# Transformer layer on one core: one pair of k tiles of the up-projection as seven products instead of eight, with weight sums built by DMA

## The chip, the cores and the metric

The kernel runs on one core of a Trainium2 chip. The metric is the device time of one execution in microseconds, the median of three runs; lower is better.

## What is computed

One layer over 256 tokens of width 2048: RMSNorm and one input projection, sixteen attention heads in two kinds, an output projection with residual, and a gated MLP with a causal depthwise convolution of width 3 between up-projection and activation. The change lies in the MLP's first product, `h @ w_up`:

```
def conv_ffn(x, norm2_g, w_up, conv_w, conv_b, w_down):
    h = rms_norm(x, norm2_g)
    u = h @ w_up                      # (256 x 2048) @ (2048 x 11008)
    u = conv over the tokens, width 3, per column, + conv_b
    gate, val = jnp.split(u, 2, axis=-1)
    return x + (jax.nn.silu(gate) * val) @ w_down
```

## The kernel before

All weights stream through one ring. A piece is 128 rows (one k tile) of up to 1024 float32 columns, 512 KB. SyncE (SP) loads it into one of four slots of `raw`; ScalarE copies it, rounded, to `w_hi` (`split_hi`); VectorE writes the rest to `w_lo` (`split_lo`); TensorE multiplies high by high, high by low and low by high, three matmuls for each product of a 128x128 block of tokens with 512 columns. Four counters order this. SP loads piece g once piece g-4 is split (`split_done`). ScalarE copies piece g once TensorE has used piece g-4 (`piece_used`). VectorE follows ScalarE, and TensorE waits for `split_done`. Each engine runs its instructions in the order in which they are written.

The pieces come in this order: 128 of the input projection, eight for each of the sixteen heads (2 x 384 columns each); 32 of the output projection; then the up-projection in eleven batches. A batch is four tiles of the gate columns and four of the value columns, 512 + 512 columns in a piece, and runs over 16 k tiles; the eleventh has 384 + 384. For each piece TensorE does 2 token blocks (m) x 2 column halves (gate, value) x 3 = 12 matmuls of 512 columns, into four PSUM banks. The banks alternate between two sets of four (`UP_BANKS`), by the batch's parity. Batches 3 to 8 run in a hardware loop, the others are written out.

While TensorE works on batch nb, ScalarE and VectorE also finish batch nb-1, by a list of steps in which step s also splits piece s+4: ScalarE takes the four banks to `ut` scaled by the norm `r2` (`evacuate_up`, steps 0 and 1), VectorE transposes 32x32 blocks (`turn_up`, steps 1 and 2), ScalarE moves them to their place (`move_up`, 16 instructions, steps 2 to 9), then both do the convolution (`conv_tap2`, `conv_taps`), silu and gate times value. The down-projection follows, which already takes nine pairs of its pieces as seven products, with sums built on VectorE.

GpSimd (POOL) is used for a few small operations in the first heads and has issued no DMA.

## Time and profile before

| | |
|---|---|
| median of 3 runs | 1038.23 us (1037.99 to 1040.0) |
| the profiled execution, its own time | 1039.86 us |
| its span in the profile | 1038.1 us |
| TensorE busy | 99% of the span |
| VectorE, ScalarE busy | 77%, 77% |
| GpSimd busy | 2% |
| granted TensorE clock | 1.0 throughout |
| moved by DMA | 221.04 MB, mean 213 GB/s |

A matmul's record is longer than the step from one to the next, since they are pipelined; the step is read from the starts. The same holds a little for ScalarE and VectorE. Times inside the span count from its start.

### The profile page before, as it was taken

The page shows a single profiled execution, that of the slowest core. Times are in us where ns is not written, and L with a number is a line of the kernel's source. Part 1 is how long each engine was busy: PE and PEld are TensorE (multiplying, and loading weights), DVE is VectorE, ACT ScalarE, POOL GpSimd, SP SyncE. Part 2 cuts the span into 40 slices and gives each one's busy share as a digit, 9 for nine tenths or more (in the row PEclk, how much of TensorE's full clock was granted, in tenths as well). Part 3 has the DMA queues.
Part 4 walks back from the last instruction along what each step waited for, and adds up shares of the span by engine and source line. Part 5 has one row for each costly group of instructions (what it writes and reads, how often), then busy time and mean ns, then how long its engine had stood idle before and what let it go on. Part 6 is the DMA issues. An engine that isn't in the chain of part 4 may idle for free.

```text
span 1038.1 us, 16517 instructions
## 1 busy us (share of the span) xinstructions
PE 1031.2 (99%) x5278; PEld 931.9 (90%) x5278; DVE 801.3 (77%) x1354; ACT 799.7 (77%) x1406; POOL 21.1 (2%) x27
## 2 busy tenths in 40 slices
PE   9999999999999999999999999999999999999998
PEld 8999999999988888888888888888889988888887
DVE  7788888878766655577776776777768799989988
ACT  7776676888858885879788788797887789856753
POOL 0101010000000000000000000000000000000000
PEclk9999999999999999999999999999999999999999
DMA  9666777777766666666565565665656757656664
GB/s 351 240 199 212 216 239 229 222 252 227 249 229 201 205 194 201 204 213 201 189 218 195 193 221 190 213 203 188 216 187 190 232 182 233 201 200 218 203 203 162
DMA packets 81437, 221.04 MB, mean 213 GB/s; under 512 B 20312, under 2 KB 24544, under 8 KB 81248
## 3 DMA queue, kind: packets, MB, share of 16 engines
q1 hardware_dynamic: 81232, 220.07, 65.0%
q8 instruction: 34, 0.56, 0.2%
q10 hardware_dynamic: 144, 0.20, 0.1%
q14 instruction: 27, 0.22, 0.1%
HBM read 214.32 MB, written 5.91 MB: 212 GB/s over the span
## 4 chain that ended last, share of the span: by engine, by line
PE 87%; DVE 8%; DMA 2%; ACT 1%; issue 1%; SPq 0%; DVEq 0%; ACTq 0%
PE ps L714 14%; PE ps L713 14%; PE ps L712 14%; PE ps L501 7%; PE ps L503 7%; PE ps L502 7%; PE ps L741 4%; PE ps L743 4%; PE ps L742 4%; DVE w_lo L1314 3%; PE ps L691 3%; PE ps L693 3%; PE ps L692 3%; DMA raw<-in_wrest 2%; PE ps L523 1%; DVE sums_lo_t L1883 1%
## 5 line engine op out<-in xcount | busy, mean ns | idle before, releaser
L1314 DVE TENSOR_TENSOR w_lo<-raw,w_hi 128x1024 fp32r<-128x1024 f32 (+2 forms) x406 | 457.1, 1131 | 186.3 <-ACT w_hi L838 184.4
L838 ACT ACTIVATE w_hi<-raw 128x1024 fp32r<-128x1024 f32 (+2 forms) x406 | 393.4, 977 | 145.3 <-PE ps L714 53.1
L712 PE MATMUL ps<-w_hi,xs 128*128 128x512 f32 (+1 forms) x704 | 263.4, 374 | 0.0
L713 PE MATMUL ps<-w_lo,xs 128*128 128x512 f32 (+1 forms) x704 | 263.4, 374 | 0.0
L714 PE MATMUL ps<-w_hi,xs 128*128 128x512 f32 (+1 forms) x704 | 263.4, 374 | 0.0
L501 PE MATMUL ps<-w_hi,xs 128*128 128x384 f32 (+1 forms) x496 | 164.9, 332 | 0.1
L502 PE MATMUL ps<-w_lo,xs 128*128 128x384 f32 (+1 forms) x496 | 161.8, 326 | 0.0
L503 PE MATMUL ps<-w_hi,xs 128*128 128x384 f32 (+1 forms) x496 | 161.8, 326 | 0.0
L712 PEld LDWEIGHTS ps<-w_hi,xs 128*128 128x128 f32 x704 | 133.1, 189 | 17.2
L713 PEld LDWEIGHTS ps<-w_lo,xs 128*128 128x128 f32 x704 | 133.1, 189 | 17.2
L714 PEld LDWEIGHTS ps<-w_hi,xs 128*128 128x128 f32 x704 | 133.1, 189 | 17.2
L1174 ACT ACTIVATE uT<-utT 32x512 f32<-32x512 f32 (+1 forms) x176 | 109.4, 622 | 26.8 <-DVE utT L1742 22.8
L741 PE MATMUL ps<-w_hi,a_s 128*128 128x512 f32 (+1 forms) x274 | 103.7, 378 | 0.0
L742 PE MATMUL ps<-w_lo,a_s 128*128 128x512 f32 (+1 forms) x274 | 103.4, 377 | 0.0
L743 PE MATMUL ps<-w_hi,a_s 128*128 128x512 f32 (+1 forms) x274 | 103.4, 377 | 0.0
L501 PEld LDWEIGHTS ps<-w_hi,xs 128*128 128x128 f32 x496 | 93.7, 189 | 2.6 <-issue 1.3
L502 PEld LDWEIGHTS ps<-w_lo,xs 128*128 128x128 f32 x496 | 93.8, 189 | 0.2
L503 PEld LDWEIGHTS ps<-w_hi,xs 128*128 128x128 f32 x496 | 93.7, 189 | 0.0
L741 PEld LDWEIGHTS ps<-w_hi,a_s 128*128 128x128 f32 x274 | 51.8, 189 | 8.0 <-issue 0.8
L743 PEld LDWEIGHTS ps<-w_hi,a_s 128*128 128x128 f32 x274 | 51.8, 189 | 7.3
L742 PEld LDWEIGHTS ps<-w_lo,a_s 128*128 128x128 f32 x274 | 51.8, 189 | 7.1
L691 PE MATMUL ps<-w_hi,mixed 128*128 128x512 f32 x128 | 49.0, 383 | 0.0
(231 smaller groups left out, 1139.1 us busy)
## 6 DMA issues: line engine op xcount, KB each, us to landing
raw<-in_wrest SPq DMA_DIRECT2D x278, 512.0 KB, 4.0
raw<-in_win SPq DMA_DIRECT2D x117, 384.0 KB, 3.6
raw<-in_wrest SPq DMA_DIRECT2D x16, 384.0 KB, 3.1
p_scratch<-pdT SPq DMA_DIRECT2D x14, 192.0 KB, 2.9
p_read<-p_scratch SPq DMA_DIRECT2D x56, 48.0 KB, 2.8
xtok<-in_xtok SPq DMA_DIRECT2D x4, 512.0 KB, 13.2
xv<-in_xtok SPq DMA_DIRECT2D x4, 512.0 KB, 5.6
raw_ahead<-in_w SPq DMA_DIRECT2D x5, 392.0 KB, 8.1
```

Source lines behind the costliest of these rows:

```text
L501: pe.matmul(o, xh, wh, start=(kt == 0), stop=False, skip_group_check=True)
L502: pe.matmul(o, xh, wl, start=False, stop=False, skip_group_check=True)
L503: last = pe.matmul(o, xl, wh, start=False, stop=(kt == KT - 1), skip_group_check=True)
L712: pe.matmul(o, xh, wh, start=(k == 0), stop=False, skip_group_check=True)
L713: pe.matmul(o, xh, wl, start=False, stop=False, skip_group_check=True)
L714: last = pe.matmul(o, xl, wh, start=False, stop=(k == KT - 1), skip_group_check=True)
L741: pe.matmul(to, ah, wh, start=start, stop=False, skip_group_check=True)
L742: pe.matmul(to, ah, wl, start=False, stop=False, skip_group_check=True)
L743: return pe.matmul(to, al, wh, start=False, stop=stop, skip_group_check=True)
L838: act.activation(slot(w_hi, s, w), slot(raw, s, w), ACT.Copy).then_inc(hi_ready, 1)
L1174: act.activation(dst, src, ACT.Copy).then_inc(u_moved, 1)
L1314: dve.tensor_tensor(slot(w_lo, s, w), slot(raw, s, w), f32(slot(w_hi, s, w)), ALU.subtract).then_inc(split_done, 1)
```

## The change

In batches 1 to 8 of the up-projection, k tiles 8 and 9 are no longer multiplied as eight blocks (2 token blocks x 2 k tiles x 2 column halves) but as seven products of sums of blocks, as in Strassen's scheme. In place of two pieces of 1024 columns there are four: `left` (the left half of tile 8, 512 columns), `lower` (tile 9), and `two` and `more`, 2 x 1024 columns of sums of the weight blocks. The sums of the token blocks are the same for all batches; they are made once, in batch 0 (`h_sums`), in `kept_hi` and `kept_lo`. The weight sums are built in a DRAM scratch tensor `t_scratch` by DMAs that GpSimd issues: per batch six, each waiting for the one before (three copies and three that add to what is there). They begin when 96 pieces are used, that is with head 12, and build q (for batch q+1) also waits for 96 + 12 q used pieces. SP waits for build q (`t_built`) before it loads piece `two` of batch q+1.

Three of the seven products go into the batch's own banks; the four that belong to more than one block go to the other set of four banks. Those are read out and combined while TensorE goes on with tiles 10 to 15: ScalarE copies the first (`take_first`), VectorE does four additions (`up_sums`), ScalarE scales the result (`scale_sums`). At the batch's end VectorE takes the four own banks out with the scale and adds these (`evacuate_sums`, a `scalar_tensor_tensor`), where ScalarE did it before. The lists of steps for ScalarE and VectorE in these batches are new (`UP_ACT`, `UP_DVE`), with 18 steps instead of 16. TensorE waits for the combined sums (`c_summed`) before the next batch, and for the evacuation of the batch before (`u_evac`) ahead of tile 8. Semaphores of two norms are shared (`norm_*`) to make room, with no other effect.

```
+UP_SEVEN, UP_BATCHES = (8,), (1, 8)
+UP_ACT = dict(late_silu=5, moves=(3, 3, 4, 4, 6, 8, 10, 10), first=9, scale=(14, 16), taps=(11, 12, 15, 16), silu=(13, 17, 17))
+UP_DVE = dict(late_taps=(3, 6), late_gate=(4, 8), evacuate=(0, 0), turn=(1, 1), sums=(9, 10),
+              taps=((11, 12), (14, 14), (16, 16)), gate=(15, 16))
+BUILD_AT = 8 * (H + 4)
...
 # SP
+            def up_pieces(nb, par):
...
+                    if kind in ("two", "more"):
...
+                        if kind == "two":
+                            sp.wait_ge(t_built, 96 * (q + 1))
+                        sp.dma_start(slot(raw, s), t_d[q * P:(q + 1) * P, c:c + PW]).then_inc(raw_landed[s], 16)
 # TensorE
+            def up_seven(nb, par, k, j):
...
+                if first:
+                    pe.wait_ge(u_evac, nb * 4)
...
+                pe.wait_ge(split_done, up_first(nb) + (j + 1))
+                product(shared[0], a(0, 0), b(0, 0), first, last).then_inc(piece_used, 1)
+                pe.wait_ge(split_done, up_first(nb) + (j + 2))
+                product(own[0], a(1, 0), b(1, 0))
+                product(own[1], a_sum(3), b(1, 1)).then_inc(piece_used, 1)
+                pe.wait_ge(split_done, up_first(nb) + (j + 3))
+                product(shared[2], a_sum(1), b(2, 0), first, last)
+                product(shared[3], a_sum(0), b(2, 1), first, last).then_inc(piece_used, 1)
+                pe.wait_ge(split_done, up_first(nb) + (j + 4))
+                end = product(shared[1], a_sum(2), b(3, 0), first, last)
+                if last:
+                    end.then_inc(c_ended, 1)
+                product(own[2], a(1, 1), b(3, 1)).then_inc(piece_used, 1)
 # ScalarE
+            def take_first(nb, par):
+                act.wait_ge(c_ended, nb)
...
+                act.activation(c_tile(0, 0), bank(UP_BANKS[1 - par][0]), ACT.Copy).then_inc(c_first, 1)
+            def scale_sums(nb, m):
+                act.wait_ge(c_summed, nb * 4)
+                act.activation((x1sq, x1f)[m][:], (x1sq, x1f)[m][:], ACT.Copy, scale=r2[:, m:m + 1]).then_inc(c_scaled, 1)
 # VectorE
+            def evacuate_sums(pb, m, par):
+                dve.wait_ge(piece_used, up_first(pb) + UP_LONG)
+                dve.wait_ge(c_scaled, pb * 2 + (m - 1))
+                dve.wait_ge(u_turned, pb * 2)
+                for gv in range(2):
+                    at = (2 * m + gv) * UW
+                    dve.scalar_tensor_tensor(out=ut[:, at:at + UW], in0=bank(UP_BANKS[par][2 * m + gv]), scalar=r2[:, m:m + 1],
+                                             in1=c_tile(m, gv), op0=ALU.mult, op1=ALU.add).then_inc(u_evac, 1)
 # GpSimd
+            def build_sums(q):
...
+                pool.dma_start(block_(0, 2), upper).then_inc(t_built, 16)
+                pool.wait_ge(t_built, 96 * q + 16)
+                pool.dma_start(block_(0, 2).rearrange("p (k c) -> p k c", k=2), both[:, :, BLOCK:PW], accum_op=ALU.add,
+                               max_dma_last_dim=4096).then_inc(t_built, 16)
...
+            for q in range(UP_SUMS):
+                pool.wait_ge(piece_used, BUILD_AT + q * 12)
+                build_sums(q)
```

How the order of instructions moves, first on VectorE at the start of a batch (the static part before the loop). `w_lo` rows are `split_lo`, `utT` the transposes. Before, batch 2:

```order
L1314 TENSOR_TENSOR w_lo<-raw,w_hi 128x1024 [waits hi_ready]
L1749 SCALAR_TENSOR_TENSOR y_t<-uT,conv,y_t 128x256 [waits g_y2]
L1754 SCALAR_TENSOR_TENSOR y_t<-uT,conv,y_t 128x256 [waits g_silu,g_y1]
L1314 TENSOR_TENSOR w_lo<-raw,w_hi 128x1024 [waits hi_ready]
L1742 STREAM_TRANSPOSE utT<-ut 128x1024 [waits u_moved,u_evac]
L1314 TENSOR_TENSOR w_lo<-raw,w_hi 128x1024 [waits hi_ready]
L1742 STREAM_TRANSPOSE utT<-ut 128x1024 [waits u_moved,u_evac]
```

After the change, from the end of batch 1 (the first `w_lo` of the two) into batch 2:

```order
L1492 TENSOR_TENSOR w_lo<-raw,w_hi 128x1024 [waits hi_ready] x2
L2024 SCALAR_TENSOR_TENSOR ut<-ps,r,x1sq 128x512 [waits u_turned,c_scaled,piece_used]
L2024 SCALAR_TENSOR_TENSOR ut<-ps,r,x1sq 128x512
L2024 SCALAR_TENSOR_TENSOR ut<-ps,r,x1f 128x512 [waits u_turned,c_scaled,piece_used]
L2024 SCALAR_TENSOR_TENSOR ut<-ps,r,x1f 128x512
L1492 TENSOR_TENSOR w_lo<-raw,w_hi 128x1024 [waits hi_ready]
L1920 STREAM_TRANSPOSE utT<-ut 128x1024 [waits u_moved,u_evac] x2
```

The four read-outs of PSUM have come to VectorE behind the first split of the batch, and both transposes stand behind the second.

GpSimd before the change had no DMA; after it, its program ends with 48 of these rows, here the first build and the start of the second (`t_scratch` is the DRAM tensor of sums):

```order
L2278 DMA t_scratch<-in_wrest 128x1024 [waits piece_used]
L2280 DMA t_scratch<-in_wrest 128x2x512 [waits t_built]
L2283 DMA t_scratch<-t_scratch 128x512 [waits t_built]
L2285 DMA t_scratch<-in_wrest 128x512 [waits t_built]
L2287 DMA t_scratch<-t_scratch 128x512 [waits t_built]
L2289 DMA t_scratch<-in_wrest 128x512 [waits t_built]
L2278 DMA t_scratch<-in_wrest 128x1024 [waits piece_used,t_built]
```

Each of the six waits for the one before it, so the builds are one chain that shares the DMA engines with the loads of SP.

## Rows read from the trace of the kernel before

**Rows 1.** Page, part 1: busy us (share of the span) xinstructions

```profile
PE 1031.2 (99%) x5278; PEld 931.9 (90%) x5278; DVE 801.3 (77%) x1354; ACT 799.7 (77%) x1406; POOL 21.1 (2%) x27
```

**Rows 2.** Page, part 4: the chain that ended last, shares by engine

```profile
PE 87%; DVE 8%; DMA 2%; ACT 1%; issue 1%; SPq 0%; DVEq 0%; ACTq 0%
```

**Rows 3.** Busy time by window: last heads, output projection, one up-projection batch

```profile
core 0: us, PE busy (x) PEld busy (x) DVE busy (x) ACT busy (x) POOL busy (x), PEclk, DMA share, GB/s
217.00:285.00 68.00, 68.00 (x420) 67.56 (x419) 53.05 (x123) 59.03 (x142) 0.00 (x0) 1.00 0.73 238
285.00:370.40 85.40, 85.40 (x404) 74.88 (x403) 54.93 (x76) 65.00 (x115) 0.00 (x0) 1.00 0.63 207
...
535.00:576.30 41.30, 41.30 (x193) 36.15 (x192) 29.73 (x38) 34.17 (x49) 0.00 (x0) 1.00 0.62 205
```

**Rows 4.** One matmul line of the up-projection: duration ns, first and last start

```profile
L712 PE MATMUL ps<-w_hi,xs x704: 326/379/379, 370.4 to 815.5; 128*128 128x512 f32 x160, 128*128 128x384 f32 x16
```

**Rows 5.** Timeline of TensorE: in head 12, and in an up-projection batch

```profile
228.84 0.59 PE L564 MATMUL ps<-p_read,qkv 128*128 128x256 f32 x2
...
547.81 0.38 PE L712 MATMUL ps<-w_hi,xs 128*128 128x512 f32 x1
...
555.80 0.38 PE L713 MATMUL ps<-w_lo,xs 128*128 128x512 f32 x1
```

**Rows 6.** Timeline of ScalarE in a batch, two instructions that follow each other

```profile
549.07 1.06 ACT L838 ACTIVATE w_hi<-raw 128x1024 fp32r<-128x1024 f32 x1
550.04 0.40 ACT L1192 ACTIVATE silu_t<-y_t 128x256 f32<-128x256 f32 x1
```

**Rows 7.** Groups of ScalarE, 535 to 577 us: count, busy, mean ns, idle before

```profile
L1174 ACT ACTIVATE uT<-utT 32x512 f32<-32x512 f32 x16 | 10.1, 631 | 2.9 <-DVE utT L1742 2.6
L1182 ACT ACTIVATE y_t<-uT,conv 128x256 f32<-128x256 f32 x10 | 5.5, 586 | 0.0
L1159 ACT ACTIVATE ut<-ps,r 128x512 f32<-128x512 f32 x4 | 2.5, 678 | 0.0
L1192 ACT ACTIVATE silu_t<-y_t 128x256 f32<-128x256 f32 x4 | 1.6, 401 | 0.0
```

**Rows 8.** Timeline of VectorE in a batch, four that follow each other

```profile
571.65 1.22 DVE L1314 TENSOR_TENSOR w_lo<-raw,w_hi 128x1024 fp32r<-128x1024 f32 x1
572.78 0.48 DVE L1749 SCALAR_TENSOR_TENSOR y_t<-uT,conv,y_t 128x256 f32<-128x256 f32 x1
573.40 0.48 DVE L1754 SCALAR_TENSOR_TENSOR y_t<-uT,conv,y_t 128x256 f32<-128x256 f32 x1
573.80 1.22 DVE L1314 TENSOR_TENSOR w_lo<-raw,w_hi 128x1024 fp32r<-128x1024 f32 x1
```

**Rows 9.** Groups of VectorE, 535 to 577 us

```profile
L1742 DVE STREAM_TRANSPOSE utT<-ut 128x1024 f32<-128x1024 f32 x2 | 2.5, 1238 | 0.0
L1762 DVE TENSOR_TENSOR a_all<-silu_t,y_t 128x256 f32 x4 | 1.7, 418 | 0.1
```

**Rows 10.** Groups from 815 us on that read PSUM, of VectorE and of ScalarE

```profile
L1920 DVE TENSOR_TENSOR sums_t<-ps,sums_t 128x512 f32<-128x512 f32 x2 | 1.4, 684 | 0.0
...
L1289 ACT ACTIVATE sums_t<-ps 128x512 f32<-128x512 f32 x2 | 1.2, 576 | 0.0
```

**Rows 11.** DMA issues of the whole run: count, KB each, median us to landing

```profile
p_scratch<-pdT SPq DMA_DIRECT2D x14, 192.0 KB, 2.9
...
xtok<-in_xtok SPq DMA_DIRECT2D x4, 512.0 KB, 13.2
...
cbc<-c_scratch SPq DMA_DIRECT2D x1, 1024.0 KB, 5.0
```

**Rows 12.** DMA issues of 215 to 286 us, then of 452 to 783 us

```profile
raw<-in_win SPq DMA_DIRECT2D x28, 384.0 KB, 3.4
...
raw<-in_wrest SPq DMA_DIRECT2D x122, 512.0 KB, 3.7
```

**Rows 13.** DMA rate in 40 slices of the first 25 us

```profile
GB/s 0 0 29 149 370 305 206 223 323 341 363 408 354 368 381 378 406 401 405 412 417 402 426 418 397 408 409 407 399 404 419 405 419 383 405 412 395 379 426 415
```

More of the change, by code:

```diff
@@ L286, in x1_block, with with_sums, up_first, up_parts @@
             return xT[:, m * D + o * PW + blk * BLOCK + at:m * D + o * PW + blk * BLOCK + at + n]
+        def with_sums(nb):
+            return not isinstance(nb, int) or UP_BATCHES[0] <= nb <= UP_BATCHES[1]
+        def up_first(nb):
+            if not isinstance(nb, int):
+                return nb * UP_LONG + (UP0 + KT - UP_LONG)
+            return UP0 + KT * nb + (UP_LONG - KT) * min(max(nb - UP_BATCHES[0], 0), UP_BATCHES[1])
+        def up_parts(nb):
+            if not with_sums(nb):
+                return [("piece", k) for k in range(KT)]
+            parts = []
+            for k in range(KT):
+                if k in UP_SEVEN:
+                    parts += [(kind, k) for kind in ("left", "lower", "two", "more")]
+                elif k - 1 not in UP_SEVEN:
+                    parts.append(("piece", k))
+            return parts
+        def up_job(part):
+            kind, k = part
+            return {"piece": k, "left": k, "two": k + 1}.get(kind)
+        def up_at(nb, par, j):
+            if isinstance(nb, int):
+                return up_first(nb) + j
+            return UP0 + KT + (0 if par else UP_LONG) + j
+        def up_round(nb, par, j, turn):
+            g = up_at(nb, par, j) // RING + 1
+            return g if isinstance(nb, int) else turn * (UP_LONG // 2) + g
+        def up_width(nb, j, ahead):
+            parts = up_parts(nb)
+            if j >= len(parts):
+                return 2 * ahead
+            if isinstance(nb, int) and nb == FULL:
+                return 2 * LW
+            return BLOCK if parts[j][0] == "left" else PW
+        def c_tile(m, gv):
+            return (x1sq, x1f)[m][:, gv * BLOCK:(gv + 1) * BLOCK]
+        def h_sum(n, i, h):
+            return (kept_hi, kept_lo)[h][:, n * BLOCK + i * P:n * BLOCK + (i + 1) * P]
         def shared_bank(o, i):
@@ L722, in up_batch @@
                     pe.wait_ge(u_evac, nb * 4 - 4)
-                for k in range(KT):
+                if not isinstance(nb, int) or UP_BATCHES[0] < nb <= UP_BATCHES[1] + 1:
+                    pe.wait_ge(c_summed, nb * 4 - 4)
+                for j, (kind, k) in enumerate(up_parts(nb)):
                     if isinstance(nb, int) and nb == 0:
                         pe.wait_ge(h2_ready, k + 1)
-                    up_piece(nb, k, UP_BANKS[par], w)
+                    if kind == "piece":
+                        up_piece(nb, par, k, j, w)
+                    if kind == "left":
+                        up_seven(nb, par, k, j)
             for nb in range(3):
@@ new lines, in up_batch @@
+            def up_batch(nb, par, post=True, spill=True, ahead=UW, last=False, turn=None):
+                for j, part_ in enumerate(up_parts(nb)):
+                    s = up_job(part_)
+                    split_hi(up_first(nb) + (j + 4), up_at(nb, par, j + 4) % RING, up_round(nb, par, j + 4, turn),
+                             up_width(nb, j + 4, ahead))
+                    if with_sums(nb):
+                        up_long_steps(nb, j, par, spill)
+                        continue
+                    if not post and 10 <= s < 10 + len(UP_SEVEN):
+                        h_sums_hi(s - 10)
@@ new lines, in up_long_steps @@
+            def up_long_steps(nb, j, par, spill):
+                pb, at = nb - 1, UP_DVE
+                for m in range(M):
+                    if with_sums(pb) and j == at["evacuate"][m]:
+                        evacuate_sums(pb, m, 1 - par)
+                    if j == at["turn"][m]:
+                        turn_up(pb, m, UW)
+                for n in range(2):
+                    if spill and j == at["late_taps"][n]:
+                        conv_taps(nb - 2, 3, n == 0, par, BATCH)
+                    if spill and j == at["late_gate"][n]:
+                        gate_times_value(nb - 2, 2 + n)
+                    if j == at["sums"][n]:
+                        up_sums(nb, par, n)
+                for t in range(3):
+                    for n in range(2):
+                        if j == at["taps"][t][n]:
+                            conv_taps(pb, t, n == 0, 1 - par, BATCH)
+                for t in range(2):
+                    if j == at["gate"][t]:
+                        gate_times_value(pb, t)
```

177 lines of the change are left out of this document (147 added, 30 removed).

## The prediction, made before the changed kernel had run

> **What bounds the kernel now.** I read the page's shares first: TensorE is busy for 1031.2 of 1038.1 us, VectorE and ScalarE for 77% [rows 1]. The chain that ended last is TensorE for 87%, with 8% of VectorE, which lies in the down-projection's end [rows 2]. By windows, TensorE is busy for the whole of the last heads, of the output projection and of a batch of the up-projection, while VectorE has work for 29.7 and ScalarE for 34.2 of a batch's 41.3 us [rows 3]. So up to the down-projection every matmul costs its step. From 547.81 to 555.80 us stand 38 matmuls of 512 columns, 37 steps of 0.216 us [rows 5]; the same comes out of the up-projection as a whole, which runs from 370.4 to 815.5 us [rows 4]. A batch is 192 steps, 41.4 us.
>
> What could hide a loss or cause one is how late the other engines may be, so I need their own pace in a batch. ScalarE's copy of a piece takes 0.97 us from start to start [rows 6]. VectorE's remainder takes 1.13 us, and two convolution steps together 1.02 us [rows 8].
>
> **What goes.** Eight products of three matmuls become seven: three matmuls fewer in each of eight batches, 24 x 0.216 = 5.2 us. Nothing else is taken from TensorE. It gains two waits on `split_done` per batch and waits on `c_summed` and `u_evac`; I take a wait that is already met at nothing, since the 37 steps measured span three piece boundaries with such waits and still come to 0.216 us each [rows 5]. The down-projection's order is the same, and what it waits for is its own, so an earlier start moves its end by as much.
>
> **What is added on the two elementwise engines, per batch.** Pieces: 17.5 instead of 16 in units of 1024 columns (one is a half). ScalarE: 17.5 x 0.97 = 17.0; the moves 16 x 0.65 = 10.4; eight taps at 0.54 and four silus at 0.40, 5.9 (their means are 586 and 401 ns, the tails overlap) [rows 7]; it loses the four evacuations, and gains one read of a bank at 0.6 [rows 10] and two scalings of 1024 columns at about 1.0, as a copy. Together 35.9 us of the new batch's 189 x 0.216 = 40.8. VectorE: 17.5 x 1.13 = 19.8; eight tap pairs 8.2; transposes 2.5, gate times value 1.7 [rows 9]; four sums and four evacuations of 512 columns, of which at least one operand is in PSUM, at 0.60 to 0.68 [rows 10], 5.1. Together 37.3 of 40.8 us. The trace has no `scalar_tensor_tensor` that reads PSUM in 512 columns. Below it I put 0.6, above it 0.96 (twice the 0.48 of 256 columns [rows 8]); I take 0.65, since the addition that reads PSUM is the nearest row. At 0.96 VectorE would have 38.5 us, still under 40.8. So neither engine is the bound by its sum; what is left is the order.
>
> **The tight place.** The seven products shorten pieces 8 to 11 of a batch to 3, 6, 6 and 6 matmuls. Count from the batch's start. Slot 11 comes free when piece 7 is used, at 96 x 0.216 = 20.7 us, and TensorE wants piece 11 after 111 matmuls, at 23.9. In between lie a copy and a remainder, 2.1 us: 1.1 us to spare. Piece 12 comes free at 99 steps (21.4), waits for ScalarE's copy of 11, is copied at 22.6 and finished at 24.0; wanted at 117 steps, 25.2: 1.2 to spare. Piece 13: free at 22.6, but two moves (1.3 us) stand before its copy, so it is finished at 26.1 and wanted at 27.8. This holds if VectorE is free at 21.7. From the batch's start to there it has seven splits (one a half, 7.4), evacuations 2.6, transposes 2.5, two tap pairs 2.0 and one gate 0.4, 14.9 us, and can begin at about 4 us with what the last batch left over; it fits with some 3 us. `take_first` waits for the product that ends at 114 steps, 24.6 us. ScalarE would be there at 24.9, so the wait costs it nothing; behind it stand the copy of piece 14 and four moves, and piece 14 is wanted at 30.4 and split by 28.5. I cost this at 0 to 0.2 us a batch and take 0.05, 0.4 us in all. In batch 9, which has the old list with VectorE's evacuation at its head, the moves begin some 4 us later than the copy before them and pieces 7 and 8 have about 1 us to spare: nothing, or some tenths.
>
> **The builds.** Head 12 begins 72 matmuls before 228.84 us; at 68 us for 420 of them [rows 3, 5] that is 11.7 us, so at 217.1. Their duration is not in the trace, which has no accumulating and no DRAM-to-DRAM DMA. From below, four of 256 KB like the 192 KB store, 2.9, and two of 512 KB like a load, 3.7: 19 us a build. From above, six like the 512 KB loads of the crowded start, 13.2: 79 us [rows 11, 12]. I take 5.0 each, the 1 MB read from scratch, as they come one at a time: 30 us. Then build 7 is ready at 217 + 240 = 457 us. It is needed in batch 8, which starts at 370.4 + 41.4 + 7 x 40.8 = 697.4; its tenth piece is wanted 105 matmuls on, at 720.0, less remainder, copy and landing at 713.9. The builds may so take up to 62 us each before SP waits and everything behind it. The Trainium skill, DMA: Bandwidth & Descriptors, "Anatomy of one DMA", fits a DMA from this queue as 2.0 us plus bytes over 436 GB/s; that would make an estimate of 17 us a build, and the same end.
>
> **The loads beside them.** A build moves 2.1 MB and re-reads half: at 30 us, 70 GB/s, with the re-reads 105, on top of 238 in the last heads [rows 3]. The engines moved some 410 GB/s when they were full [rows 13]. What a slower load costs: slot g is loaded after split g-4, so four pieces can't take less than issue, landing, copy and remainder. In the heads four pieces last 8.5 us, their parts without landing 2.1, so a landing of up to 6.4 us costs nothing, against 3.4 now; in the up-projection 9.1 and 2.4, up to 6.6, against 3.7 [rows 12]. Cost nothing, if a load beside a build lands less than 3 us later.
>
> **Sum.** -5.2 + 0.4 = -4.8 us, on the profiled execution 1039.86 to 1035.1 (span 1038.1 to 1033.3). The median of the runs is 1.6 us below that execution, so 1038.23 - 4.8 = 1033.4.
>
> **Rivals.**
> *Late in the seven products* (14%). If the read-out of PSUM or the waits behind it are slower than I take them, VectorE reaches piece 11 late in every batch. Each batch then loses 0.2 to 0.65 us, in all 1.6 to 5.2: 1034.6 to 1038.3. For it: VectorE at 91%, 1.1 us to spare. Against it: the sums above.
> *Partly crowded loads* (15%). The heads and batch 1 run beside the builds, and a landing of 7 us costs 0.6 us for each four pieces. Over eight groups in the heads and some in batch 1, 1 to 5 us: 1034.4 to 1038.
> *Fully crowded loads, slower* (5%). If each load beside a build lands as in the first 25 us, at about 8.5, four pieces in the heads last 10.6 instead of 8.5. With the ring's lead of some 6 us gone, eight groups lose 17 - 6 = 11 us, 1045. It decides from a landing of 6.4 + 0.6 = 7.0, where the loss equals the gain.
> *Late builds, slower* (6%). From 62 us each the end moves by 8 us for each us more; the gain is gone at 62.7. At 79 it would be 135 us, 1169. A mechanism that could bring this: GpSimd's DMAs start only when VectorE is idle. VectorE is busy for 53 of the 68 us of four heads [rows 3]; if each DMA waited out one head's work, 13.3 us, a build would take 6 x 18.3 = 110 us, build 7 would be ready at 1097, and the time would be near 1417. I give that 1 of the 6 in 100; nothing in the trace speaks for so long a wait. By the Trainium skill, SBUF — State Buffer, "SBUF: two separate sides" (the "DVE blocks DMA" trap), the descriptors of a DMA issued from GpSimd can't be written while VectorE runs an operation in a mode that takes both ports, and one such DMA took five times as long. By that rule with the page's five times on the estimate of 17 us, a build would take 85 us and the time would be near 1216, an estimate; but the page names copies and one-operand operations for that mode, and nearly all of VectorE's rows here have two operands, so the trace speaks for the small chance.
> *It does nothing* (6%): if VectorE were the bound of a batch at 41.4 us, the three matmuls would turn into a wait; 1038.
>
> **Chances and range.** A measurement of this kernel tells 0.2%, 2.1 us, from no change. The forecast, 1032.8 to 1034.4, has 54%. Faster: 54 + 7 of the first rival + 11 of the second = 72%. Same: 5 + 3 + 6 = 14%. Slower: 2 + 1 + 5 + 6 = 14%. The range runs from 1032.7 (all of 5.2, and a little of the runs' own spread) to 1037.6, which takes in most of the first two rivals.
>
> **What would show it.** In the trace after: 189 matmuls in 40.8 us in batches 2 to 8 and no gap of TensorE around the seven products; idle time of VectorE for ScalarE in a batch down to about 3 us; the builds in a chain of about 30 us each, the last before 500 us; loads landing under 6 us beside them; SP with no wait for `t_built`. I would be wrong by a gap ahead of pieces 11 or 12, by landings over 6.4 us in the heads, or by an SP that waits at piece 10.

## The result, and the profile after

The changed kernel takes 1057.93 us (median of 4 runs, 1053.93 to 1059.86), the kernel before beside it 1038.28 us: a ratio of 1.0181 [1.0149, 1.0213]. It is slower by 1.8%, where the forecast was 1033.4 us. The profiled execution is the quickest of the four, 1053.93 us with a span of 1052.1, 14.1 us over the profiled one of before; what follows accounts for these 14.1 us. Its four runs lie up to 6 us apart, and only this one was traced.

The page of the kernel after, parts 1, 3, 4 and 6 (for parts 1 and 4 the rows of before are [rows 1, 2]):

```profile
PE 1032.4 (98%) x5254; PEld 928.9 (88%) x5254; DVE 854.5 (81%) x1440; ACT 811.1 (77%) x1415; POOL 57.1 (5%) x75
...
q1 hardware_dynamic: 83536, 226.36, 64.8%
q0 software_dynamic: 6912, 16.78, 8.4%
...
PE 48%; DVE 20%; DMA 12%; ACT 11%; issue 7%; SPq 1%; DVEq 1%; ACTq 0%
...
t_scratch<-in_wrest POOLq DMA_DIRECT2D x16, 512.0 KB, 7.5
...
t_scratch<-t_scratch POOLq DMA_DIRECT2D x16, 256.0 KB, 4.8
t_scratch<-in_wrest POOLq DMA_DIRECT2D x16, 256.0 KB, 7.4
```

The 24 matmuls are gone (5254 instead of 5278), yet TensorE's busy time rose by 1.2 us, so some matmuls became longer. The chain is the first thing to read: TensorE held 87% of it and now holds 48%, and DMA went from 2 to 12%. A kernel that was bound by TensorE now waits for data in between.

Busy time of the kernel after in windows: the last heads, the output projection, one batch's time of the up-projection beside builds, and 100 us of it behind the builds ([rows 3] for before):

```profile
core 0: us, PE busy (x) PEld busy (x) DVE busy (x) ACT busy (x) POOL busy (x), PEclk, DMA share, GB/s
217.00:285.00 68.00, 62.15 (x370) 61.00 (x369) 48.42 (x110) 52.72 (x126) 8.45 (x12) 0.97 0.88 261
285.00:370.40 85.40, 83.28 (x396) 73.29 (x395) 54.83 (x83) 60.84 (x110) 9.32 (x13) 0.98 0.86 257
...
494.60:536.00 41.40, 40.08 (x185) 34.44 (x184) 35.62 (x47) 34.49 (x48) 4.47 (x6) 1.00 0.88 264
600.00:700.00 100.00, 98.98 (x457) 85.73 (x456) 86.43 (x113) 85.51 (x119) 0.00 (x0) 1.00 0.65 217
```

In the heads TensorE is idle for 5.9 of 68 us and its granted clock is 0.97 of full. The DMA engines are busy for 0.88 of the window, against 0.73, and yet move only 261 GB/s, against 238: the share grew by 21%, what it moved by 10%.

Where the 14 us are is read from the first start of three matmul lines, the output projection's (`mixed`), the up-projection's and the down-projection's (`a_s`). Before, then after:

```profile
L691 PE MATMUL ps<-w_hi,mixed x128: 379/379/567, 284.8 to 369.7; 128*128 128x512 f32 x128
L741 PE MATMUL ps<-w_hi,a_s x274: 273/379/455, 816.0 to 1033.8; 128*128 128x512 f32 x135, 128*128 128x256 f32 x2
```

```profile
L776 PE MATMUL ps<-w_hi,mixed x128: 379/379/774, 291.9 to 380.9; 128*128 128x512 f32 x128
L871 PE MATMUL ps<-w_hi,a_s x274: 273/379/456, 830.0 to 1047.8; 128*128 128x512 f32 x135, 128*128 128x256 f32 x2
```

The same rows of every run give this table, in us of the profiled execution (the down-projection is the rest of the span):

| kernel | heads end | output proj. | up-proj. | down-proj. |
|---|---|---|---|---|
| before | 284.8 | 85.6 | 445.6 | 222.1 |
| after | 291.9 | 89.7 | 448.4 | 222.1 |
| e1 no builds | 284.7 | 85.6 | 444.0 | 222.2 |
| e2 builds alone | 295.5 | 91.7 | 445.6 | 221.3 |
| e3 builds behind the heads | 286.6 | 85.7 | 457.6 | 221.8 |
| e4 plain copies | 294.2 | 85.6 | 445.0 | 221.6 |
| e5 no builds, taps earlier | 283.8 | 85.6 | 444.0 | 221.2 |
| e6 builds alone, behind the heads | 284.6 | 85.6 | 446.2 | 220.4 |
| e7 four batches | 284.9 | 85.6 | 443.0 | 220.8 |
| e8 six batches | 284.9 | 85.6 | 443.4 | 220.5 |
| e9 no builds, written out, taps earlier | 285.9 | 85.6 | 441.0 | 220.5 |
| e10 no builds, written out | 284.6 | 85.7 | 441.0 | 221.2 |
| e11 builds alone, values later | 294.7 | 89.1 | 445.6 | 220.8 |
| e12 before, values later | 284.9 | 85.6 | 445.6 | 221.6 |
| e13 written out, builds behind the heads | 283.5 | 85.6 | 453.9 | 220.5 |
| e14 changed kernel, written out | 293.9 | 90.4 | 443.8 | 220.5 |

The change lost 7.1 us in the heads and 4.1 in the output projection, where not one matmul was edited, and another 2.8 in the up-projection, where 5.2 should have been gained. Of the 11.2 us ahead of the up-projection TensorE is idle for 8.0 (5.9 in the heads, 2.1 in the output projection), and its waits for one tile, `p_read`, make up these 8.0: 4.6, 1.3 and 2.1 us. The other 3.2 are in longer steps, most of them behind the waits of 4.6 and 2.1, where the granted clock was lower.

What TensorE waits for in the heads is in the chain of waits of the kernel after, from 218 us (start, us, what):

```profile
218.34 0.59 DVE pdT L1619
...
218.95 4.93 DMA p_scratch<-pdT
...
223.89 0.33 SPq L460
...
225.22 7.26 DMA p_read<-p_scratch
...
232.60 0.73 PE ps L649 x2
```

The probabilities of a head make a round trip through DRAM: VectorE turns them (`pdT`), SP stores them to `p_scratch`, waits for the landing, and reads them back as `p_read`; TensorE multiplies them with the values at piece 5 of the next head. Here the two transfers took 4.9 and 7.3 us. In SP's timeline of the kernel before, one head:

```profile
236.57 0.33 SPq L385 DMA_DIRECT2D p_scratch<-pdT  x1
...
239.94 1.75 SPq L395 DMA_DIRECT2D p_read<-p_scratch  x4
```

The store is issued at 236.57, the last read starts at 241.3 and takes the median 2.7 us, and TensorE uses the result at 245.8: under 2 us to spare, behind two transfers in series, the store (median 2.6 us) and the read. Nothing waited there, so no view of waits named it. TensorE's timeline after that wait, in the kernel after:

```profile
232.60 0.73 PE L649 MATMUL ps<-p_read,qkv 128*128 128x256 f32 x2 [4.59 <-DMA p_read<-p_scratch]
...
235.47 0.53 PE L588 MATMUL ps<-w_hi,xs 128*128 128x384 f32 x1
235.79 0.53 PE L586 MATMUL ps<-w_hi,xs 128*128 128x384 f32 x1
...
236.65 0.33 PE L586 MATMUL ps<-w_hi,xs 128*128 128x384 f32 x1
236.81 0.33 PE L587 MATMUL ps<-w_lo,xs 128*128 128x384 f32 x1
```

Behind the idle 4.59 us a step of 384 columns is 0.32 us from start to start, and from 236.65 on it is 0.16: at first the lower of the clock's two levels (1.2 GHz), then the upper (2.4 GHz); over the 4.05 us from 232.60 on the granted clock is 0.58 of full. A stall can so cost more than itself: the heads have 5.9 us of idle time and lost 7.1, the output projection has 2.1 and lost 4.1. Not every wait does this. Behind the 2.1 us at 308.3 in this kernel the clock fell too (0.50 of full from 309 to 311), behind the 1.3 us at 269.7 it did not, and behind one of 3.2 us in e11 (at 312.1) the step stayed at 0.216 us.

GpSimd's timeline of the first build (the bracket is the idle time before an issue, and what ended it):

```profile
216.62 0.75 POOL L2278 DMA_DIRECT2D t_scratch<-in_wrest  x1 [60.77 <-PE ps L588]
223.40 1.21 POOL L2280 DMA_DIRECT2D t_scratch<-in_wrest  x1 [6.02 <-DMA t_scratch<-in_wrest]
...
256.45 0.54 POOL L2278 DMA_DIRECT2D t_scratch<-in_wrest  x1 [7.60 <-DMA t_scratch<-in_wrest]
```

A build takes 39.8 us (216.62 to 256.45), and eight of them last to about 542 us. That is in time for every batch: SP has no wait for `t_built` in the trace.

The waits of the kernel after, the rows that matter (us in total, times, longest):

```profile
PEld ps L820 <- DVE w_lo L1492: 9.0, 9, 2.6
PE ps L649 <- DMA p_read<-p_scratch: 8.0, 3, 4.6
PEld ps L649 <- issue: 6.4, 2, 4.9
...
PE ps L820 <- DVE w_lo L1492: 5.7, 8, 2.2
```

`p_read` three times, and line 820, the seven products, in eight places: pieces that VectorE has not finished. Read from the starts, the three at 488, 528 and 532 us, beside builds, cost 4.3 us with the longer step behind each, and the five at 573 to 739 us, one a batch and behind all builds, cost 3.5. Together that is 7.8 of the 8.0 us by which the up-projection misses its 440.4 (445.6 less 5.2).

### The profile page after: what moved, and what is told of

It is laid out like the page before. It is cut to its first block, busy times and chain, and to the rows that moved or that the text cites. A ratio compares the mean times of both kernels' runs of the same rounds, so it can differ in the third digit from the quotient of the medians.

```text
span 1052.1 us, 16316 instructions
## 1 busy us (share of the span) xinstructions
PE 1032.4 (98%) x5254; PEld 928.9 (88%) x5254; DVE 854.5 (81%) x1440; ACT 811.1 (77%) x1415; POOL 57.1 (5%) x75
## 3 DMA queue, kind: packets, MB, share of 16 engines
q0 software_dynamic: 6912, 16.78, 8.4%
## 4 chain that ended last, share of the span: by engine, by line
PE 48%; DVE 20%; DMA 12%; ACT 11%; issue 7%; SPq 1%; DVEq 1%; ACTq 0%
DVE w_lo L1492 8%; DMA raw<-in_wrest 5%; PE ps L798 5%; PE ps L800 5%; PE ps L799 5%; PE ps L871 4%; PE ps L873 4%; PE ps L872 4%; ACT w_hi L968 4%; PE ps L586 4%; PE ps L587 3%; PE ps L588 3%; ACT uT L1306 3%; DMA raw<-in_win 2%; PE ps L776 2%
## 5 line engine op out<-in xcount | busy, mean ns | idle before, releaser
L1492 DVE TENSOR_TENSOR w_lo<-raw,w_hi 128x1024 fp32r<-128x1024 f32 (+2 forms) x422 | 469.6, 1123 | 146.1 <-ACT w_hi L968 143.2
L968 ACT ACTIVATE w_hi<-raw 128x1024 fp32r<-128x1024 f32 (+2 forms) x422 | 406.5, 972 | 157.8 <-DMA raw<-in_wrest 38.6
L798 PE MATMUL ps<-w_hi,xs 128*128 128x512 f32 (+1 forms) x640 | 239.3, 374 | 0.0
L799 PE MATMUL ps<-w_lo,xs 128*128 128x512 f32 (+1 forms) x640 | 239.2, 374 | 0.0
L800 PE MATMUL ps<-w_hi,xs 128*128 128x512 f32 (+1 forms) x640 | 239.2, 374 | 0.0
L798 PEld LDWEIGHTS ps<-w_hi,xs 128*128 128x128 f32 x640 | 121.0, 189 | 16.0 <-DVE w_lo L1492 0.4
L800 PEld LDWEIGHTS ps<-w_hi,xs 128*128 128x128 f32 x640 | 121.0, 189 | 15.4
L799 PEld LDWEIGHTS ps<-w_lo,xs 128*128 128x128 f32 x640 | 121.0, 189 | 15.4
L586 PEld LDWEIGHTS ps<-w_hi,xs 128*128 128x128 f32 x496 | 94.1, 190 | 3.3 <-DVE w_lo L1492 1.7
L587 PEld LDWEIGHTS ps<-w_lo,xs 128*128 128x128 f32 x496 | 94.1, 190 | 0.2
L588 PEld LDWEIGHTS ps<-w_hi,xs 128*128 128x128 f32 x496 | 94.0, 190 | 0.0
```

Source lines behind the costliest of these rows:

```text
L586: pe.matmul(o, xh, wh, start=(kt == 0), stop=False, skip_group_check=True)
L587: pe.matmul(o, xh, wl, start=False, stop=False, skip_group_check=True)
L588: last = pe.matmul(o, xl, wh, start=False, stop=(kt == KT - 1), skip_group_check=True)
L798: pe.matmul(o, xh, wh, start=(k == 0), stop=False, skip_group_check=True)
L799: pe.matmul(o, xh, wl, start=False, stop=False, skip_group_check=True)
L800: last = pe.matmul(o, xl, wh, start=False, stop=(k == KT - 1), skip_group_check=True)
```

## The experiments

The kernel before that each ratio is taken against ran on the same chip: 1039.36 us for e1 to e4, 1038.78 for e5 to e8, 1039.07 for e9 to e12, 1038.87 for e13 and e14.

**e1, no builds.** The seven products as they are, with no build on GpSimd; SP loads rows of the weights in place of the sums, which are so other data.

```diff
-                        if kind == "two":
-                            sp.wait_ge(t_built, 96 * (q + 1))
-                        sp.dma_start(slot(raw, s), t_d[q * P:(q + 1) * P, c:c + PW]).then_inc(raw_landed[s], 16)
+                        row = (UP0 - IN_PIECES + nb * KT + k + (kind == "more")) * P
+                        sp.dma_start(slot(raw, s), wrest_d[row:row + P, :]).then_inc(raw_landed[s], 16)
...
-            for q in range(UP_SUMS):
-                pool.wait_ge(piece_used, BUILD_AT + q * 12)
-                build_sums(q)
```

> The changed kernel without GpSimd's DMAs: the pieces `two` and `more` are loaded from the input weights (so the sums are wrong numbers), with the same sizes and the same order, and SP has no wait for t_built. Theory A (the builds crowd out the loads and the attention's way through DRAM; the seven products by themselves are free): 1033 to 1035 us, a gain of 3.5 to 5.2 on the kernel before, and TensorE has no wait in the heads. Rival B (the seven products come late for VectorE and ScalarE in every batch): 1048 us or more.

Measured: 1037.76 us against 1039.36, ratio 0.9982 [0.9973, 0.9992]. The whole loss of the heads and the output projection is gone with the builds, but the up-projection gained only 1.6 of 5.2 us. What is left stands in the waits of e1:

```profile
PE ps L819 <- DVE w_lo L1491: 1.8, 6, 0.4
```

Six batches have a gap ahead of piece 11, the tight place, with nothing beside them.

**e2, the builds alone.** The kernel before, plus `t_scratch`, `t_built` and the loop over `build_sums` from head 12 on; no batch uses the sums.

> The kernel before with the eight builds added on GpSimd, with the same waits, and nobody reads what they build. Theory A: slower than before by 12 to 20 us, 1050 to 1058, with some 10 of it ahead of 381 us and with waits of TensorE for p_read. Rival B: 1038 to 1040.

Measured: 1054.92 us, ratio 1.0135 [1.011, 1.0161]. The waits of e2:

```profile
PE ps L568 <- DMA p_read<-p_scratch: 12.2, 5, 4.3
```

The builds alone cost 10.7 us in the heads and 6.1 in the output projection. TensorE is idle for 8.8 and 3.9 of these, nearly all for `p_read`; the other 4.1 us are in longer steps, the clock's share among them. Its plain batches of the up-projection, with builds beside them up to 541 us, took 445.6 us as before: the same traffic costs nothing there.

**e3, builds behind the heads.** The changed kernel with the builds from the last head's last piece on, issued from 311 to 623 us.

```diff
-BUILD_AT = 8 * (H + 4)
+BUILD_AT = 8 * (H + 9)
```

> The changed kernel with BUILD_AT = 136 in place of 96: the builds begin behind the last head's values, in the output projection, and end at about 626 us, ahead of every use (build 7 is wanted at 714). Theory A: the 7 us of the heads and the 2 us at the first output pieces come back, while more batches run beside builds, at 1 to 2 us each: 1040 to 1047. If the crowding of the weights' loads alone were the cause, wherever it falls: no change, 1055 to 1058. Rival B: 1057.

Measured: 1052.02 us, ratio 1.0115 [1.0099, 1.0132]. Heads and output projection are free of loss, and the up-projection takes 457.6 us, 17 more than its 440.4. From 410 to 620 us weight pieces land in 5.4 us (DMA issues of e3: KB each, median us to landing):

```profile
raw<-in_wrest SPq DMA_DIRECT2D x71, 512.0 KB, 5.4
raw<-t_scratch SPq DMA_DIRECT2D x10, 512.0 KB, 6.4
```

The time is above the forecast of theory A, 1040 to 1047 us, and below the 1055 of the rivals. The prediction allowed landings of 6.6 us at no cost; these medians keep to it, but the longest landing was 8.5. The bound counted a ring of four that only refills, and left out what the copy then meets on ScalarE and VectorE.

**e4, plain copies.** The changed kernel with `accum_op` taken from the three accumulating DMAs of a build; the sums so hold copies of one block.

```diff
-                pool.dma_start(block_(2), lower[:, BLOCK:PW], accum_op=ALU.add, max_dma_last_dim=4096).then_inc(t_built, 16)
+                pool.dma_start(block_(2), lower[:, BLOCK:PW]).then_inc(t_built, 16)
```

> The changed kernel with the three accumulating DMAs of each build as plain copies of the same sizes (so the sums are wrong numbers). If it is the accumulating that loads the DMA engines (it reads its target too): builds of 25 us instead of 40, and 1036 to 1042. If the bytes moved and the chain's presence in the heads do it: 1048 or more. Rival B: 1057.

Measured: 1047.11 us, ratio 1.0067 [1.0051, 1.0084]. A build takes 33 us instead of 40, GpSimd's queue 5.1% of the engines' time instead of 8.4% for the same 16.78 MB, and the output projection loses nothing. The profiled execution still lost 9.4 us in the heads, so plain copies are enough for that loss. The time lies between its forecasts (1036 to 1042, and 1048 or more). By the medians accumulating makes some 12 of the 21 us that the builds cost: the ratios are 1.0181 with it, 1.0067 with plain copies and 0.9982 without builds (e1).

**e5, taps earlier.** As e1, and `late_taps=(3, 4)` in place of `(3, 6)`: the two tap pairs that stand at place 6 move ahead by two pieces.

> The kernel of e1 (no builds, sums from the input weights) with VectorE's second late tap pair at step 4 instead of 6, so that nothing stands between the remainders of pieces 10 and 11. Theory C (the 3.3 us that e1 lost of its 5.2 are waits for piece 11 behind that tap pair): 1034 to 1035.5 us where the kernel before has 1038.3, and no wait of TensorE for the pieces of the seven products. Rival D (VectorE and ScalarE are late by their sums, not by this pair): the same as e1, 1036.5.

Measured: 1037.72 us against 1038.78, ratio 0.9988 [0.9978, 0.9997]; the up-projection took 444.0 us as in e1, with the same six gaps. The theory that this tap pair makes VectorE late fell.

**e6, builds alone, behind the heads.** e2 with `BUILD_AT = 8 * (H + 9)`.

> The kernel before with the eight builds on GpSimd from piece 136 on, behind the last head's values. Theory A now says that the builds cost only where TensorE waits for the attention's way through DRAM or for a piece of the seven products, and neither is there: 1038 to 1039, the same as before. If crowded weight loads cost by themselves: 1043 or more.

Measured: 1038.87 us, ratio 1.0 [0.9991, 1.0009]. Beside the output projection and plain batches eight builds cost nothing that the runs can tell. (The 0.6 us of the table are six steps of the up-projection, 0.05 to 0.1 us longer each, between 557 and 599 us.) So neither the number of builds nor their traffic is the price; it is what stands beside them.

**e7, four batches, builds first.** Batches 5 to 8 alone as seven products, builds behind the heads (308 to 468 us, done before they are needed), taps as in e5. The counts of the waits depend on the first such batch, so the loops over batches are written out. The sums are the built ones.

```diff
-UP_SEVEN, UP_BATCHES = (8,), (1, 8)
+UP_SEVEN, UP_BATCHES = (8,), (5, 8)
...
-            with dve.Fori(1, 4) as i:
+            for i in range(1, 4):
```

> Seven products in batches 5 to 8 only, four builds from piece 136 on (about 306 to 466 us, ahead of batch 5 at 577), the tap pair of e5, and the loops over batches written out so that batches can differ. Theory A with C: no wait of TensorE, 4 x 0.65 = 2.6 us gained, 1035.7 (1035 to 1037). If the seven products lose also without builds beside them and with the pair moved: 1037.5 or more.

Measured: 1036.22 us, ratio 0.9977 [0.9968, 0.9986], faster than both kernels. The up-projection is shorter by 2.6 us, which is 4 x 0.65, all of what twelve matmuls are worth, and there is no gap at piece 11. So twelve matmuls less are worth their steps with real sums. Like e1 it has no build beside its seven products; what else differs from e5, the same taps with gaps, is the loops and the number of such batches, and e9 parts these two.

**e8, six batches.** As e7 with `(3, 8)`; the builds last to 549 us and stand beside its first two such batches.

> The same with batches 3 to 8, six builds (about 306 to 546 us), so that batch 3 and the start of batch 4 run beside builds. Theory A: 6 x 0.65 = 3.9 gained, less 1 to 3 us in batch 3: 1035 to 1038. If builds beside seven products cost nothing: 1034.4.

Measured: 1036.65 us, ratio 0.9978 [0.9969, 0.9988]. Of 3.9 us the up-projection gave 2.2; TensorE waited for 0.8 us at the seven products of batch 4, at 561 us, just behind the last builds. That is inside its forecast of 1035 to 1038, and no better than four batches.

**e9 and e10, all eight batches without builds, loops written out.** The kernels of e5 and e1 with the one edit to the loops, so that the waits are against constants; e10 has the taps where the changed kernel has them. The sums are other data again.

> The changed kernel without the GpSimd builds (the rows that held sums are loaded from the weights instead, so the sums are other data), as in the kernel of e5 with the two taps of the next batch at places 3 and 4, and now with the loops over the up-projection's batches written out, so that VectorE's, ScalarE's and TensorE's waits in them are against constants. Theory R (waits against register values make VectorE and ScalarE late for piece 11, which costs 0.5 to 0.6 us in six batches of eight): no gap ahead of piece 11, up-projection 440.4 us long, 1033.5 us in all (-5.2). Theory T (the order of eight batches of seven products in a row is too tight for the copies whatever the waits): gaps as in e5, up-projection 444.0, 1037.5 us.

> As e9, with the two taps of the next batch where the changed kernel has them, at places 3 and 6. Theory R: the written-out waits alone give the slack back, 1033.5 us, no gap. Rival S (the tap at place 6 stands in VectorE's way too, so that both edits are needed): a gap of 0.1 to 0.4 us ahead of piece 11 or 12 in most batches, up-projection 441 to 443 us, 1034 to 1036.5 us.

Measured: e9 1034.36 us, ratio 0.995 [0.9936, 0.9963]; e10 1033.69 us against 1039.07, ratio 0.9945 [0.9931, 0.9958]. The up-projection took 441.0 us in both, and no wait for VectorE stands in the seven products but one of 0.3 us. The taps make no difference. Where this comes from is seen on VectorE, in the same batch of e1 and of e10 (L1926 and L1931 are the two steps of a tap pair, the second needs the first's result). e1, in the loop:

```profile
618.90 0.48 DVE L1926 SCALAR_TENSOR_TENSOR y_t<-uT,conv,y_t 128x256 f32<-128x256 f32 x1
619.52 0.48 DVE L1931 SCALAR_TENSOR_TENSOR y_t<-uT,conv,y_t 128x256 f32<-128x256 f32 x1
619.92 0.48 DVE L1926 SCALAR_TENSOR_TENSOR y_t<-uT,conv,y_t 128x256 f32<-128x256 f32 x1
...
623.55 1.41 DVE L2023 SCALAR_TENSOR_TENSOR ut<-ps,r,x1sq 128x512 f32<-128x512 f32 x2
```

e10, written out:

```profile
616.98 0.48 DVE L1926 SCALAR_TENSOR_TENSOR y_t<-uT,conv,y_t 128x256 f32<-128x256 f32 x1
617.49 0.48 DVE L1931 SCALAR_TENSOR_TENSOR y_t<-uT,conv,y_t 128x256 f32<-128x256 f32 x1
617.89 0.48 DVE L1926 SCALAR_TENSOR_TENSOR y_t<-uT,conv,y_t 128x256 f32<-128x256 f32 x1
...
621.41 1.41 DVE L2023 SCALAR_TENSOR_TENSOR ut<-ps,r,x1sq 128x512 f32<-128x512 f32 x2
```

The instructions are as long, 0.48. The second of a pair starts 0.62 us after the first in the loop and 0.51 written out, while the step behind it comes 0.40 later in both: it is the instruction that waits for a result just made that starts 0.11 us later. The kernel before shows the same within one run: the pair is 0.51 us apart in the batches ahead of the loop and behind it, and 0.62 or more in it. The evacuation (L2023) then begins 6.3 us into the batch in e1 (which starts at 617.29) and 5.2 in e10 (616.25), and what follows it is as much later, ScalarE's moves among it (L1305), which wait for VectorE's transposes in e1 and not in e10:

```profile
629.85 2.59 ACT L1305 ACTIVATE uT<-utT 32x512 f32<-32x512 f32 x4 [0.95 <-DVE utT L1919]
```

```profile
627.84 2.59 ACT L1305 ACTIVATE uT<-utT 32x512 f32<-32x512 f32 x4
```

They begin 12.6 us into the batch in e1, 11.6 in e10, and the copies of pieces 10 and 11 queue behind them. TensorE's timeline at piece 11, e1, then e10:

```profile
640.60 0.38 PE L819 MATMUL ps<-w_hi,kept_hi 128*128 128x512 f32 x1
641.79 0.48 PE L819 MATMUL ps<-w_hi,kept_hi 128*128 128x512 f32 x1 [0.38 <-DVE w_lo L1491]
```

```profile
639.56 0.38 PE L819 MATMUL ps<-w_hi,kept_hi 128*128 128x512 f32 x1
640.21 0.38 PE L819 MATMUL ps<-w_hi,kept_hi 128*128 128x512 f32 x1
```

Three steps take 1.19 us in e1 and 0.65 in e10: the wait of 0.38 costs 0.54 with the restart. Six such batches, 3.2 us, are most of the 3.6 that e1 missed; e10 misses 0.6.

**e11 and e12, the values one piece later.** The builds alone (as e2), and the kernel before, both with `block_values` and the two mixes behind it one piece later in heads 10 to 15. This gives the round trip through DRAM another 1.7 us.

```diff
-                    if spill and b == 5:
+                    if spill and b == 6:
                         block_values(f - 1, par)
```

> The kernel before with the eight builds from head 12 (as e2), and the products of the probabilities with the values, which wait for p_read, one piece later in heads 10 to 15 (about 1.7 us more for the bounce through DRAM). Theory B (what the builds cost in the heads is the wait for p_read, and the slow clock behind it): the wait of five heads shrinks by 1.7 us each and the clock falls less often, first out-projection product at 286 to 290 us instead of 295.5, 1044 to 1050 us instead of 1054.9. Rival L (later weight pieces cost it, and p_read only shows them): first out-projection product stays at 293 to 296 us, 1053 to 1056 us.

> The kernel before with only the move of e11 and no builds: what the move costs or gives by itself. Both theories: within 0.5 us of the kernel before (1038.8), since the bounce has 1.5 to 1.9 us to spare there; if it is slower by more, e11 is to be read against this run.

Measured: e12 1039.45 us, ratio 1.0006 [0.9997, 1.0015], so the move by itself is free. e11 1053.01 us, ratio 1.0146 [1.0127, 1.0166], no better than e2, and its heads end at 294.7 us: both numbers lie in the forecast of rival L and outside that of theory B. In e11 between 217 and 300 us TensorE waits for

```profile
PE ps L505 <- DVE w_lo L1318: 5.2, 4, 2.0
...
PE ps L568 <- DMA p_read<-p_scratch: 1.0, 1, 1.0
```

The wait for `p_read` fell from 8.5 us in this window of e2 to 1.0, and waits for the heads' own weight pieces took its place; the heads end at 294.7 us instead of 295.5, though the granted clock was 1.00 throughout. In the output projection the wait for `p_read` stayed, 3.2 of the 3.5 us lost there. Behind the late pieces is the spread of the landings: in e11 the pieces of these 75 us landed in 3.2 to 9.3 us, median 5.4. The same of the kernel after, 26 pieces of `w_in` and five of `w_out` from 217 to 292 us (in the kernel before the median was 3.7 and the longest 6.4):

```profile
DMA to landing us min/median/max: 3.1/4.5/9.6
```

The median stays well under the forecast's bound of 6.4 us and the longest goes over it by 3. So my theory that the round trip is the loss fell: it is the wait that ends last in e2, but with it gone late pieces cost nearly as much. So the two seem to have nearly the same slack. A third thing may be in both: SP issues in order, and it waited for the landing of `p_scratch` for 6.9 us in e2 and 5.2 in e11 in this window, with loads of weight pieces behind it. No run takes this wait away.

**e13 and e14, with builds, written out.** e3 and the changed kernel, with nothing edited but the loops.

> The kernel of e3 (all eight batches as seven products, builds from the last head on, behind its last piece) with the loops over batches written out, so that the waits are against constants; all sums are real. Written-out waits gave 3.6 us of slack back where there were no builds (e10 against e1). Theory M (two causes that add up: late waits from registers, and landings of 5 to 6 us beside the builds): up-projection some 3.6 us shorter than in e3 (454 instead of 457.6), 1048 us. Theory N (the landings only hurt because the slack had been used up by the register waits): gaps ahead of pieces 8 to 12 all but gone, up-projection 441 to 444 us, 1034 to 1037 us.

> The changed kernel itself, with nothing edited but the loops over the up-projection's batches, written out. What the builds cost in heads 12 to 15 and the out-projection (11 us in the profiled run) stays under each theory. Theory M: the gaps behind batch 3 vanish (about 2.4 us) and those of batches 2 and 3, where builds still run, stay, 1053 to 1056 us. Theory N: the up-projection falls to 440.4 to 441.5 us, 1050 to 1052 us.

Measured: e13 1045.13 us, ratio 1.0058 [1.0044, 1.0073]. Its up-projection takes 453.9 us, 3.7 less than e3 and 13.5 over the ideal, where theory M, that the two causes add up, said 454. (In the profiled executions the rest of the difference is 3.1 us ahead of the output projection, where e3 waited 2.4 us for its first weights and e13 0.2, and 1.3 in the down-projection.) e14 1056.98 us, ratio 1.0178 [1.0161, 1.0195], which the runs can't tell from the changed kernel, and slower than both forecasts. Its traced execution is the quickest of five, 1050.43 us; there the up-projection took 443.8 us instead of 448.4, its three gaps at line 820, 2.0 us in all, lie between 480 and 545 us, beside the builds, and none is left behind them, as theory M said. In the total this gain does not show: the heads lost 9.1 us here and the output projection 4.8. The slack that the written-out waits give back doesn't cover a late landing.

## Why the prediction was wrong

The forecast for the profiled execution was -4.8 us, and it came to +14.1. Of these 18.9 us 11.2 lie in the heads and the output projection, 4.3 in the gaps of the up-projection beside builds, and 3.1 in the gaps behind them (3.5, where the forecast had 0.4).

**-5.2 us for 24 matmuls: right in size, under a condition.** The step of 0.216 us and the count held: 2.6 of 2.6 us in e7, 4.6 of 5.2 in e10. A matmul less is worth its step where the pieces are there.

**"Cost nothing, if a load beside a build lands less than 3 us later": the step that failed, and the larger part.** It costed every load by the slack of the weight ring, by medians, and no other transfer at all. Three things were missing. First, the round trip `pdT`, `p_scratch`, `p_read` stands between VectorE and TensorE in every one of these heads, and it had under 2 us to spare with two transfers in series. I had its store among the DMA rows as a price for the builds [rows 11] and its matmul as a mark in the timeline [rows 5], and never asked how long before its use it landed. Second, the bound of 6.4 us was set against a median: for the pieces of `w_in` it moved from 3.4 [rows 12] to 4.8 us in the same window, and single landings went to 9.6. Third, idle TensorE came back at half the clock for some 3 us, behind two of three waits. In place of 0 the heads and the output projection cost 11.2 us in the profiled run (8.0 idle, 3.2 in longer steps), the up-projection beside the builds another 4.3, and e2 without any of the rest 16.8. The rival *partly crowded loads* named this traffic at 1 to 5 us in heads and batch 1; it had the traffic and under half of the size, and it priced the ring's loads, not the round trip that ended last.

**"They come one at a time: 30 us" a build: 40 measured.** Line by line, with medians of eight, the 512 KB copy (L2278) landed in 6.7 us and the 512 KB accumulating DMA (L2280) in 8.7; the page's 7.5 is the two together. The 256 KB accumulating DMAs took 7.4 and the 256 KB copies 4.8, where I took 5.0 for each of the six. It was inside the bounds (19 to 79), and for lateness it changed nothing: limit 62, no wait for `t_built`. But it kept the builds beside the seven products of batches 2 and 3, until 542 us instead of 457. The page of the Trainium skill that I weighed, DMA: Bandwidth & Descriptors, "Anatomy of one DMA", gave 17 us a build as an estimate; the trace has 40, so the trace disagrees by more than twice, beside other traffic and with three of six accumulating (33 us with plain copies, e4). Of the "DVE blocks DMA" trap (SBUF — State Buffer, "SBUF: two separate sides") nothing is seen in the instructions themselves: GpSimd's DMA instructions take 0.54 to 1.21 us, with VectorE 71% busy. Whether a part of the landings is such a wait no run shows.

**"0.05, 0.4 us in all" for late waits: the second step that failed; 3.6 measured without a build (e1), 3.5 behind the builds in the changed kernel, and 17 with the builds moved beside more such batches (e3).** The place was named rightly, piece 11. "It fits with some 3 us" was the error: VectorE's evacuation was taken to begin about 4 us into the batch and began at 6.3, which took 2.3 of the 3 us. The rest went on a chain that I had not costed: late transposes make ScalarE's moves late, the moves stand before the copies of pieces 10 and 11, and VectorE waits for these. Of the 2.3 us 1.1 is the loop's: the six tap pairs ahead of it, at 0.11 us each, make 0.7, and the rest was there before them. The tap pair at 1.02 us was read from the loop of before [rows 8], so this price was in my sum; what I did not do is lay out the last batch's steps up to the evacuation in their order, one by one. The rival *late in the seven products* had this case, at 1034.6 to 1038.3 us, and without the builds it was the true one (e1, 1037.76).

**The interaction.** Each term was judged alone against the slack of the kernel before. The seven products use up the slack of pieces 8 to 13, and the builds stretch the landings that this slack was for. In the up-projection e6 and e2 (builds, no seven products: +0.6 and 0 us), e10 (seven products, no builds: -4.6 us) and e13 (both: +8.3 us on 445.6) show that neither costs by itself and the two together do.

What stays open: why a landing beside the builds now and then takes 9 us and not 5, whether through the order in the rings or in DRAM; why the clock fell behind a wait of 2.1 us and not behind one of 3.2; and how much of the heads' loss is SP's own wait for `p_scratch`.

## What to carry to other kernels

Before background DMAs are added, list every transfer that TensorE waits for, with the time from its landing to its use, and take round trips through DRAM with them: a view of waits shows none of them while the slack is still positive. Price them all, since taking away the wait that ends last can bring out the next one at the same cost (e11). Set the slack against the longest landing, not against the median. Put background traffic where nothing latency-bound stands beside it (e6, 0 us), and let the part that saves matmuls begin when it is over (e7, -0.23%).
